# Two transformer blocks on one core: lower activations of the feed-forwards placed 64 bytes ahead of the lower weights, modulo 256

## What is computed

```python
def swiglu(x, w_gate, w_up, w_down):                 # D_MODEL = 1024, D_FF = 2816
    return (jax.nn.silu(x @ w_gate) * (x @ w_up)) @ w_down

h = h + 0.5 * rms_norm(swiglu(rms_norm(h, pre_g), w_gate, w_up, w_down), post_g)   # feed-forwards 1 and 2

def conv_ffn(h, w_up, conv_w, w_down):               # feed-forward 3
    a, g = jnp.split(dwconv(h @ w_up, conv_w), 2, axis=-1)
    return (jax.nn.silu(g) * a) @ w_down
```

## Time and profile before

| | |
|---|---|
| median of 3 runs | 1211.1 us (1205.41 to 1211.77) |
| span of the profiled execution, first to last instruction | 1206.9 us |
| TensorE busy | 98% of the span, 9128 matmuls |
| VectorE, ScalarE, GpSimd busy | 68%, 53%, 44% |
| granted TensorE clock, mean | 0.987 |
| feed-forwards | about 10 to 197, 420 to 607 and 1019 to 1203 us of the span |

### The profile page before, as it was taken

One profiled execution on the slowest core, in us unless ns is written; L12 is line 12 of the kernel. 1 busy time (PEld: TensorE's weight loads), 2 busy tenths in 40 slices (PEclk: granted clock), 3 DMA queues, 4 the chain that ended last, 5 costly groups with the idle time before them and its releaser, 6 DMA issues.

```text
span 1206.9 us, 24404 instructions
## 1 busy us (share of the span) xinstructions
PE 1178.4 (98%) x9128; PEld 1111.1 (92%) x9128; DVE 816.0 (68%) x1121; ACT 637.3 (53%) x1018; POOL 527.1 (44%) x285
## 2 busy tenths in 40 slices
PE   6999999999999999999999999999999999999998
PEld 6999999987889899999999879987877999999998
DVE  7788875856865577777654852688836596655555
ACT  6444446525762555454546546468517635655553
POOL 0343436732465533343436645458530483232331
PEclk9999998999999999999989999999999999999999
DMA  6888884543334467878614333233323254666663
GB/s 221 277 278 294 283 280 130 190 140 123 105 108 137 157 210 259 292 274 292 188 52 158 123 99 129 88 106 105 105 70 106 88 175 140 208 185 188 188 189 121
DMA packets 58100, 207.10 MB, mean 172 GB/s; under 512 B 6576, under 2 KB 8240, under 8 KB 57776
## 3 DMA queue, kind: packets, MB, share of 16 engines
q1 hardware_dynamic: 49824, 177.23, 45.2%
q0 software_dynamic: 6912, 25.17, 5.7%
q10 hardware_dynamic: 1296, 3.74, 0.9%
HBM read 205.07 MB, written 1.05 MB: 171 GB/s over the span
## 4 chain that ended last, share of the span: by engine, by line
PE 82%; DVE 8%; issue 3%; ACT 3%; POOL 2%; DMA 1%; DVEq 0%; SPq 0%; POOLq 0%; ACTq 0%
PE psum L641 23%; PE psum L642 23%; PE psum L643 22%; POOL own_parts L2944 2%; PE psum L789 1%; PE psum L1017 1%; PE psum L942 1%; PE psum L652 1%; PE psum L654 1%; PE psum L653 1%; PE psum L666 1%; PE psum L1346 1%; POOL high L3039 1%; DVE u_parts L2882 1%; PE psum L700 1%
## 5 line engine op out<-in xcount | busy, mean ns | idle before, releaser
L641 PE MATMUL psum<-parts 128*128 128x256 f32 x1584 | 441.0, 278 | 14.0 <-DVE parts L2197 10.4
L642 PE MATMUL psum<-parts 128*128 128x256 f32 x1584 | 445.7, 281 | 0.0
L643 PE MATMUL psum<-parts 128*128 128x256 f32 x1584 | 441.6, 279 | 0.0
L641 PEld LDWEIGHTS psum<-parts 128*128 128x128 f32 x1584 | 299.5, 189 | 14.9 <-issue 11.0
L2952 POOL TENSOR_TENSOR parts<-low,parts 128x1024 fp32r<-128x1024 f32 x60 | 151.0, 2517 | 367.4 <-ACT parts L1520 367.4
L643 PEld LDWEIGHTS psum<-parts 128*128 128x128 f32 x1584 | 299.7, 189 | 0.0
L642 PEld LDWEIGHTS psum<-parts 128*128 128x128 f32 x1584 | 299.7, 189 | 0.0
L1520 ACT ACTIVATE parts<-low 128x1024 fp32r<-128x1024 f32 x198 | 207.4, 1056 | 163.1 <-DMA low<-stream 162.4
L2944 POOL TENSOR_TENSOR own_parts<-low,parts 128x1024 fp32r<-128x1024 f32 x75 | 184.9, 2479 | 151.5 <-ACT parts L1598 147.4
L2197 DVE TENSOR_TENSOR parts<-low,parts 128x1024 fp32r<-128x1024 f32 x138 | 163.6, 1219 | 23.6 <-ACT parts L1520 22.9
L642 PE MATMUL psum<-u_parts,parts 128*128 128x256 f32 (+1 forms) x560 | 164.7, 294 | 0.0
(11 more groups left out here) (384 smaller groups left out, 2091.1 us busy)
## 6 DMA issues: line engine op xcount, KB each, us to landing
low<-stream SPq DMA_DIRECT2D x334, 512.0 KB, 3.6
high<-conditioning POOLq DMA_DIRECT2D x48, 512.0 KB, 5.0
high<-wuq ACTq DMA_DIRECT2D x1, 1152.0 KB, 5.1
low<-x SPq DMA_DIRECT2D x4, 256.0 KB, 6.3
high<-ctx ACTq DMA_DIRECT2D x1, 1024.0 KB, 6.4
out<-low SPq DMA_DIRECT2D x8, 128.0 KB, 1.8
low<-cst ACTq DMA_DIRECT2D x1, 850.5 KB, 4.8
low<-vec ACTq DMA_DIRECT2D x1, 157.5 KB, 6.3
```

What stands on the lines that cost most here:

```text
L641: pe.matmul(out, w_hi[:, cols_], x_hi, start=start, stop=False, **kw)
L642: pe.matmul(out, w_hi[:, cols_], x_lo, start=False, stop=False, **kw)
L643: return pe.matmul(out, w_lo[:, cols_], x_hi, start=False, stop=stop, **kw)
```

## The change

The three tables of starts become one, for all feed-forwards. `ring_lo` stays at 16, `u_hi` and `hidden_hi` at 112. `hidden_lo` goes from 144 (208 in the third) to 128. `u_lo` goes from 16 (80 in the second and third) to 64 for chunks 3 to 7; chunks 0 to 2 of all three feed-forwards lie where those of the first did, at 16. The views lose their index k. Nothing else changes: same instructions, same order, same waits.

```diff
-PART_STARTS = ({"ring_lo": 16, "u_hi": 112, "u_lo": 16, "hidden_hi": 112, "hidden_lo": 144},
-               {"ring_lo": 16, "u_hi": 112, "u_lo": 80, "hidden_hi": 112, "hidden_lo": 144},
-               {"ring_lo": 16, "u_hi": 112, "u_lo": 80, "hidden_hi": 112, "hidden_lo": 208})
+LEVEL = 3
+PART_START = {"ring_lo": 16, "u_lo": 64, "u_hi": 112, "hidden_hi": 112, "hidden_lo": 128}
...
         def ffn_parts(name, n, width):
 
-            return [parts[:, PARTS[name][0] + starts.get(name, 0):PARTS[name][0] + starts.get(name, 0) + n * width]
-                    .rearrange("p (a b) -> p a b", a=n) for starts in PART_STARTS]
-
-        ring_hi = parts[:, 0:RING * TILE].rearrange("p (a b) -> p a b", a=RING)
-        ring_lo = ffn_parts("ring_lo", RING, TILE)
+            at = PARTS[name][0] + PART_START.get(name, 0)
+            return parts[:, at:at + n * width].rearrange("p (a b) -> p a b", a=n)
+
+        ring_hi, ring_lo = ffn_parts("ring_hi", RING, TILE), ffn_parts("ring_lo", RING, TILE)
         u_hi, u_lo = ffn_parts("u_hi", DC, T), ffn_parts("u_lo", DC, T)
+        u_lo = [parts[:, PARTS["u_lo"][0] + 16 + n * T:PARTS["u_lo"][0] + 16 + (n + 1) * T] for n in range(LEVEL)] \
+            + [u_lo[:, n, :] for n in range(LEVEL, DC)]
         hidden_hi, hidden_lo = ffn_parts("hidden_hi", 2, T), ffn_parts("hidden_lo", 2, T)
...
-                return ring_hi[:, j % RING, :], ring_lo[k][:, j % RING, :]
+                return ring_hi[:, j % RING, :], ring_lo[:, j % RING, :]
...
-                                               (u_hi[k][:, c_, :], u_lo[k][:, c_, :]),
+                                               (u_hi[:, c_, :], u_lo[c_]),
                                                c_ == 0, c_ == DC - 1)
...
-                                           (hidden_hi[k][:, par, :], hidden_lo[k][:, par, :]),
+                                           (hidden_hi[:, par, :], hidden_lo[:, par, :]),
                                            first and n % 2 == 0, last, skip_group_check=True)
```

More of the change, by code:

```diff
@@ L1505, in input_upper @@
             def input_upper(k, n, g):
[L1507 removed]
+                act.activation(u_hi[:, n, :], h[:, n, :], ACT.Identity, scale=v(g, n)).then_inc(S("input_upper"), 1)
             def uppers(k, first, last):
@@ L1525, in upper_hidden @@
                 act.wait_ge(S("hidden_ready"), count + 1)
-                act.activation(hidden_hi[k][:, par, :], hidden[:, par, :], ACT.Copy)\
+                act.activation(hidden_hi[:, par, :], hidden[:, par, :], ACT.Copy)\
                    .then_inc(S("hidden_upper"), 1)
@@ L2113, in _ @@
                 act.wait_ge(S("prescaled"), 16 + n + 1)
-                act.activation(u_hi[2][:, n, :], u1[:, n, :], ACT.Identity, bias=modc[:, 24 + n, 0:1])\
+                act.activation(u_hi[:, n, :], u1[:, n, :], ACT.Identity, bias=modc[:, 24 + n, 0:1])\
                    .then_inc(S("input_upper"), 1)
```

15 lines of the change are left out of this document (7 added, 8 removed).

## The result

The changed kernel takes 1216.8 us (median of 8 runs, 1214.0 to 1218.5) against 1210.7 (8 runs, 1205.4 to 1212.0) of the kernel before beside it: ratio 1.0064, 95% interval 1.0043 to 1.0084, about 8 us slower. The prediction was 1203.2 us: 8 us the other way. The time lies in the stated range of 1200.5 to 1220 us only because that range reached over both signs; by the forecast's own range, 1200 to 1206, it is far out.

What follows compares the result with a forecast made beforehand. TensorE's matmul spacing was taken to bound the feed-forwards. 1188 changed products at 6.7 ns less gave -7.9 us, everything else nothing: 1211.1 - 7.9 = 1203.2 us, own range 1200 to 1206, 8-in-10 range 1200.5 to 1220.

Steps and rivals of the forecast that it cites:

- What bounds the kernel: In mid feed-forward nobody holds TensorE up; time is number of matmuls by spacing, 346.7 ns a product of three.
- no place could matter: A rule against the forecast, from the Trainium skill: TensorE's two read ports are independent, so the sum would be nothing.
- Step (a): Feed-forward products with moved lower activations: 1188 changed products each 6.7 ns shorter, 7.9 us gained.
- two bounds of equal size: For the changed products, from the branch products: 7.9 us gained by the fast unit, 7.9 us lost by the slow stretch.
- What the prediction said would show it wrong: L642 shortens and L641 or L643 lengthen by as much, or TensorE begins to wait in the middle windows.
- Step (b): Writers and readers at new places (ACT L1526, DVE L2203, L2209, L2215): nothing, as later tiles cover them; L2209 bound 0.3 us.
- (c): Ring slots come free up to 2% faster behind a faster TensorE; transfers, ScalarE, GpSimd and VectorE do not become the bound.
- The half clock at nothing: Half-clock stretch after a stall: some eight products, under 0.1 us of gain left out per feed-forward.
- The median 4.2 us above the span: Median of runs lies 4.2 us above the profiled span, unaffected by the change: 1211.1 us before.
- Rival 1: Without the level pair on L642 the stream falls into the long spacing: 7.9 us lost, 1219.0 us; chance 0.27, all or part.
- Rival 2: Only L642 falls, L643 keeps 115.6 ns: 4.8 to 5.9 us gained, about 1205.8 us; chance 0.12.
- Rival 3: Nothing: the 4 ns are not from the places, or the new pair costs as much: 1211.1 us; chance 0.23.

Runs made afterwards that it cites:

- experiment 4: Kernel before with all of `parts` moved 64 bytes; feed-forwards placed as before, as the change, and with all eight `u_lo` chunks moved: 1221.5 us beside 1209.0.
- experiments 2: Kernel before with lower activations 64 bytes after lower weights, 128 after, or level with lower weights also moved, one per feed-forward: 1221.8 us beside 1209.0.
- experiment 7: Kernel before with three more placings of weights and activations, one table per feed-forward; its table collects 20 placings seen so far: 1221.6 us beside 1211.0.
- experiment 8: Kernel before with the 340 ns placing in all feed-forwards (`ring_lo` 32, `u_lo` 48, `hidden_lo` 112): 1203.3 us against 1208.2, ratio 0.9953.
- experiment 12: Kernel before with only `u_lo` chunk 3 moved in the first feed-forward, 3 and 4 in the second, 3 to 5 in the third: 1208.6 us beside 1207.7.
- experiment 1: Kernel before with `hidden_lo` alone moved in feed-forward one, `u_lo` chunks 3 to 7 in two, all chunks and `hidden_lo` in three: 1218.2 us beside 1209.0.
- experiments 3: Kernel before with the branch products' placing (-1, -1, 0) in the first feed-forward, (-1, 0, 0) in the second, (-2, 0, +1) in the third: 1216.4 us beside 1209.0.
- experiment 15: The changed kernel profiled a second time, with no edit: span 1216.1 us, feed-forwards 568.0 us.
- experiment 13: The kernel before profiled a second time, with no edit: span 1208.4 us, feed-forwards 562.1 us.

## Why the prediction was wrong, step by step

**What bounds the kernel: right.** The feed-forwards are TensorE's, time is matmuls by spacing, and the change moved spacing and nothing else. Places count: experiment 4 shows that the distances do, and absolute places don't. The Trainium skill, "SBUF — State Buffer", section "Who interferes with whom", and "TensorE: Matmul & The Clock Gate", section "Step-by-step: what each phase is for", give the streamed operand and the weight load a read port each, and say that TensorE waits for nobody and that a load takes nothing from a running matmul. If no place could matter by that, as the prediction reads it, the runs differ: the same instructions took 340 to 360 ns a product by distance alone (experiments 2, 7 and 8). Whether the two reads hold each other up, or something else does, no view shows.

**Step (a), the spacing of the changed products: the step that failed.** I had two bounds of equal size, 6.7 ns less and 6.7 more, and one row for each. I chose the lower one because L641 ran short with a one-place distance, that is, I took spacing to be a property of the pair of one line, what it streams and what is loaded meanwhile. The runs refute that. L641's pair wasn't touched and went from 113 to up to 123 ns. The unmoved chunk behind a moved one pays 12 ns (experiment 12: 123 + 121 + 114 against 346.7), and a tile behind a moved one 15 ns (experiment 1). And placings with the same pair on every line take 346.7, 353.3 and 360.0 ns (experiment 7's table). For the same reason neither bound was the change's: both came from the branch products, (-1, -1, 0), which share its pairs but not its third distance. Their two spacings are both real, as experiments 3 and 15 show, and the reason for choosing the fast one, L641's short record, doesn't tell which of them comes. The term: 1188 x -6.7 = -7.9 us was forecast, +11.0 us measured, +9.3 ns for each changed product. That is beyond the upper bound of 7.9 us too: the change's placing isn't the branches' and costs 1.8 ns more (355.1 against 353.3), and unmoved products pay as well, which a sum over the 1188 moved ones can't hold.

**What the prediction said would show it wrong** was: L642 shortens, and L641 or L643 lengthen by as much. That is what happened, except that they lengthen by far more: in the changed products L642 moved between 1.7 ns less and 0.9 more, while L641 lost up to 10 and L643 up to 7.

**Step (b), the writers, and (c), other engines as the bound: right for this change.** In the first window L2203 takes 1109 ns (1145 before), L2197 1215 (1215), L2952 2656 (2559), and TensorE's wait for L2209 is that of the earlier trace rows, 2.8 us. For a TensorE that is really faster, (c) said that none becomes the bound; in experiment 8's profile the first feed-forward was held up by VectorE and GpSimd. As experiment 13 shows the same of the kernel before, the cover worked out there is fine only in executions in which the two don't disturb each other.

**The half clock at nothing: right for the change, too narrow in view.** No effect of the change on it shows over three profiles each. But the stages outside the feed-forwards move by up to 6 us from execution to execution, some 3 of them by the clock, as much as what is asked about.

**The median 4.2 us above the span: wrong.** Every profiled execution's own time is 1.6 to 1.7 us above its span (1216.4 us to 1214.7, 1210.05 to 1208.4). The rest of the 4.2 was the spread among the runs. That spread, from the clock and the hold-up, is also the likely reason why the medians differ by 6 and the ratio by 8 us where the feed-forwards of the first two profiles differ by 11, though this is argued and not shown. Over three profiles each, with the hold-up once in before, the feed-forwards differ by 568.2 - 558.6 = 9.6 us.

**Rival 1 gave nearly the time (1219.0 us, chance 0.27), but its reason was only half right.** The changed stream does fall out of step; but a level pair isn't what keeps it in step, since (-1, 0, +2) is level and takes 360.0 ns, (-2, 0, +1) 353.3, and the fastest placing has no level pair. Its price, the branch products' 353.3 ns on the changed products alone, came so near by luck: a changed product costs more and unmoved ones pay too, 11 us in the feed-forwards of the first profiles, but the runs differ by 3 us less than that. Rival 2 (only L642 falls) is true of the first moved product and of no other. Rival 3 (nothing) is excluded: the interval of the ratio begins at 1.0043, and the spacings moved.

## What to carry to other kernels

Read matmul spacing per line and from product to product. Where one placing shows two spacings in a profile, neither is a bound for another stage until it is known what picks them; more profiles of the same kernel tell at least how often each comes (here 4 of 96 products in one and 76 of 96 in another). The distances of all streamed and loaded tensors modulo 256 bytes act together and on the matmuls that follow, so a placing is to be timed as a whole, in small steps, and never judged by the one pair that was changed. And compare stages, not spans, when the clock and a hold-up between two other engines move each execution by as much as the change.

## What the runs showed of the hardware that I had not expected

- The same 24 matmuls of a tile take 2.72 to 2.88 us (340.0 to 360.0 ns a product) by the distances of four tensors alone, and a shift of 16 bytes shows.
- A displaced product behind undisturbed ones costs nothing itself (345.0 against 346.7 ns); the ones behind it pay (358.3 and 349.9 ns in experiment 12), and it takes two undisturbed ones until the old rhythm is back.
- Two placings with the same distance between streamed and loaded operand on every line can differ by 13 ns a product (340.2 and 353.3).
- One placing can hold either of two spacings through a stretch, 340 or 353.3 ns a product, in the same code from execution to execution (the branch stage, experiment 15 against before).
- In some executions of one and the same kernel VectorE's and GpSimd's subtractions in the first feed-forward take 1.34 and 1.5 times as long (1622 against 1215 ns, 3853 against 2559), and TensorE loses 5 us. A VectorE subtraction can stand still until GpSimd's has ended (3.4 us for 1.2).
- Open: why these distances cost what they cost (no view shows what a matmul waits for within its spacing; that four spacings, 340.0, 346.7, 353.3 and 360.0 ns, lie 6.7 ns apart is a hint), the other 44 placings, what picks between the two spacings of the branch products, and what starts the hold-up.
